# Hybrid encoder trunk: row norms tile by tile with the root on GpSimd, transposes by tile, table builds behind the first rows

## What is computed

```python
def _rmsnorm(x, g, eps=EPS):
    xf = x.astype(jnp.float32)
    y = xf * lax.rsqrt(jnp.mean(xf * xf, axis=-1, keepdims=True) + eps)
    return (y * g.astype(jnp.float32)).astype(x.dtype)

for l in range(DEPTH):
    h = _rmsnorm(x, norm_mix[l])
    x = x + (_even_mixer if l == 0 else _diff_attention)(h, ...)
    h = _rmsnorm(x, norm_ffn[l])
    x = x + _hier_moe(h, ...)     # 4 groups x 8 experts, top 2 of the best group
return _rmsnorm(x, norm_final)
```

## Time and profile before

| | us |
|---|---|
| median of 3 runs | 1727.0 (1726.47 to 1728.35) |
| the profiled execution's own time | 1730.77 |
| its span, first to last instruction | 1728.7 |
| PE busy | 1449.9 (84%) |
| DVE busy | 463.4 (27%) |
| ACT busy | 540.3 (31%) |
| POOL busy | 206.6 (12%) |
| DMA | 471.47 MB, mean 273 GB/s |
| chain that ended last, shares of the span | PE 48%, DMA 37%, DVE 7%, ACT 5% |

### The profile page before, as it was taken

One profiled execution on the slowest core, in us unless ns is written; L12 is line 12 of the kernel. 1 busy time (PEld: TensorE's weight loads), 2 busy tenths in 40 slices (PEclk: granted clock), 3 DMA queues, 4 the chain that ended last, 5 costly groups with the idle time before them and its releaser, 6 DMA issues.

```text
span 1728.7 us, 26191 instructions
## 1 busy us (share of the span) xinstructions
PE 1449.9 (84%) x9958; PEld 892.8 (52%) x9959; DVE 463.4 (27%) x983; ACT 540.3 (31%) x1013; POOL 206.6 (12%) x337
## 2 busy tenths in 40 slices
PE   4998994997887887884799898794997999879992
PEld 2875584553443443441688544482554555445551
DVE  4253734110110110112433587433110111101113
ACT  3334743221121121122422377632221222212222
POOL 3020000111111111110000000000211121111110
PEclk9999996998998998997899998996998999989996
DMA  3313036899999999995232100058999989999994
GB/s 142 105 68 123 2 122 246 333 405 404 413 410 407 412 407 406 413 404 197 71 97 97 60 33 22 25 215 307 403 417 406 395 340 422 423 413 401 396 383 165
DMA packets 67299, 471.47 MB, mean 273 GB/s; under 512 B 11368, under 2 KB 12392, under 8 KB 33456
## 3 DMA queue, kind: packets, MB, share of 16 engines
q1 hardware_dynamic: 52848, 438.73, 63.6%
q0 software_dynamic: 11520, 17.34, 3.0%
q10 hardware_dynamic: 2880, 14.68, 2.1%
HBM read 465.95 MB, written 25.20 MB: 284 GB/s over the span
## 4 chain that ended last, share of the span: by engine, by line
PE 48%; DMA 37%; DVE 7%; ACT 5%; issue 2%; SPq 0%; ACTq 0%; POOL 0%; DVEq 0%; POOLq 0%
DMA w<-in_w 30%; PE bank L374 17%; PE bank L748 15%; DMA xg<-hn_dram,icol 5%; PE bank L763 4%; PE bank L564 2%; PE bank L667 2%; DVE X L1381 1%; PE bank L647 1%; ACT HN L992 1%; PE bank L728 1%; DVE HN L1049 1%; PE bank L734 1%; DVE Pm L1235 1%; ACT Pm L944 1%
## 5 line engine op out<-in xcount | busy, mean ns | idle before, releaser
L748 PE MATMUL bank<-w,xT 128*64 128x256 f32 x4480 | 540.8, 403 | 104.7 <-DMA w<-in_w 103.0
L748 PEld LDWEIGHTS bank<-w,xT 128*64 128x64 f32 x4480 | 342.0, 146 | 326.5 <-issue 189.8
L1367 DVE TENSOR_TENSOR hh<-bank,sgate 64x256 f32<-64x256 f32 x140 | 59.6, 426 | 868.9 <-ACT sgate L1009 868.9
L763 PE MATMUL bank<-w,hT 128*64 128x512 f32 x1120 | 255.8, 598 | 0.0
L1009 ACT ACTIVATE sgate<-bank 64x256 f32<-64x256 f32 x140 | 52.7, 376 | 509.9 <-PE bank L748 509.9
L763 PEld LDWEIGHTS bank<-w,hT 128*64 128x64 f32 x1120 | 74.2, 136 | 124.7 <-issue 119.9
L333 ACT ACTIVATE whi<-raw 128x512 fp32r<-128x512 f32 (+1 forms) x112 | 67.4, 615 | 169.3 <-PE bank L374 168.8
L1016 ACT ACTIVATE ysb<-bank 128x512 f32<-128x512 f32 x70 | 41.8, 597 | 237.9 <-PE bank L763 237.9
L341 DVE TENSOR_TENSOR wlo<-raw,whi 128x512 fp32r<-128x512 f32 (+1 forms) x112 | 74.7, 679 | 149.2 <-ACT whi L333 149.2
L374 PE MATMUL bank<-whi,hi 128*128 128x512 f32 x224 | 90.8, 405 | 3.6 <-DVE wlo L341 3.6
L1009 ACT ACT_TABLE_LOAD x70 | 89.8, 1283 | 1.3
(11 more groups left out here) (225 smaller groups left out, 1485.0 us busy)
## 6 DMA issues: line engine op xcount, KB each, us to landing
w<-in_w SPq DMA_DIRECT2D x192, 2048.0 KB, 32.7
raw<-in_od_w_in SPq DMA_DIRECT2D x12, 1024.0 KB, 5.1
YG<-y_dram ACTq DMA_DIRECT2D x8, 1024.0 KB, 7.9
raw<-in_ev_w_in SPq DMA_DIRECT2D x6, 1024.0 KB, 5.1
raw<-in_ev_w_out SPq DMA_DIRECT2D x4, 1024.0 KB, 5.2
hn_dram<-HN ACTq DMA_DIRECT2D x8, 512.0 KB, 7.4
raw<-in_od_w_out SPq DMA_DIRECT2D x4, 1024.0 KB, 5.1
Wb<-line_dram SPq DMA_DIRECT2D x8, 448.0 KB, 3.6
```

The costliest lines, as they stand in the source:

```text
L748: last = pe.matmul(B[(1, 4)[c]][j * SLOT:j * SLOT + SLOT, 0:HH], xT[:, k, :], W13[s][:, j, k, c * HH:c * HH + HH], start=k == 0, stop=k == ...
L763: last = pe.matmul(B[3][j * SLOT:j * SLOT + SLOT, :], hT[:, k, :], W2[s][:, k, j * 512:j * 512 + 512], start=k == 0, stop=k == FK - 1)
L1367: dve.tensor_tensor(hh[:, c * HH:c * HH + HH].rearrange("q (a p) -> q a p", a=2), B[(1, 4)[c]][SLOT:P, 0:HH].rearrange("q (p a) -> q a p", ...
```

## The change

It touches the five row norms and the start. (1) `Square` gets a scale of D to the -1/2, so that its accumulator holds the mean square. The root is formed on POOL: add 1e-6, then the power -0.5 against a tile of constants, tile by tile at the first, third and fifth norm (`row_rstd`; s_sq, s_var2, s_row1) and for four columns at once in the routers. Ln and Exp and the dummy Ln go from ScalarE. (2) VectorE normalises each tile when its own factor is there; behind the expert stages these normalises (or final products) stand inside `combine`, one tile late. (3) Transposes run tile by tile; all eight chunks of the last tile signal. (4) The first dense group of each mixer waits for max(k + 1, 4) lo chunks; the bias-line products move behind chunk 5 of group 0. (5) CT gets its own semaphore, s_ct; PE's first wait is for it alone. (6) POOL's table builds wait for all eight lo chunks, and Wd is built in four parts; lambda products and cbf copies move behind groups 0 and 1 on VectorE.

```diff
-        def dense(pe, G, hi, lo, after=None, chunk=None):
+        def dense(pe, G, hi, lo, after=None, chunk=None, first=0, base=0):
...
                 if chunk:
-                    pe.wait_ge(chunk, k + 1)
+                    pe.wait_ge(chunk, base + max(k + 1, first))
...
-            sp.dma_start(CT[:, :], consts).then_inc(s_const, 16)
+            sp.dma_start(CT[:, :], consts).then_inc(s_ct, 16)
...
-                            sp.wait_ge(s_rstd, 3)
+                            sp.wait_ge(s_row1, TT + 1)
...
-            pe.wait_ge(s_const, 32)
+            pe.wait_ge(s_ct, 16)
...
-                for k in range(KD):
-                    for t in range(TT):
-                        if k == 0:
-                            pe.wait_ge(s_hn, TT * i + t + 1)
+                for t in range(TT):
+                    pe.wait_ge(s_hn, TT * i + t + 1)
+                    for k in range(KD):
                         last = pe.transpose(B[k][:, t * P:t * P + P], HN[:, t, k * P:k * P + P], ident)
-                    last.then_inc(s_htps, 1)
+                        if t == TT - 1:
+                            last.then_inc(s_htps, 1)
...
-                pe.wait_ge(s_lo, KD)
-                pe.wait_ge(s_bkt, 16)
-                for j in range(2):
-                    pe.matmul(B[6 + j][0:8, :], par("relb")[0:32, :], bkt[:, j * 512:j * 512 + 512], start=True, stop=True
-                              ).then_inc(s_line_mm, 1)
+                def bias_line():
+                    pe.wait_ge(s_lo, KD)
+                    pe.wait_ge(s_bkt, 16)
+                    pe.wait_ge(s_const, 16)
+                    for j in range(2):
+                        pe.matmul(B[6 + j][0:8, :], par("relb")[0:32, :], bkt[:, j * 512:j * 512 + 512], start=True, stop=True
+                                  ).then_inc(s_line_mm, 1)
...
-                for G in range(4):
+                dense(pe, 0, hi0, lo0, {5: bias_line}, s_lo, 4)
+                for G in range(1, 4):
                     dense(pe, G, hi0, lo0, {3: kv_transposes} if G == 2 else None)
-                pe.wait_ge(s_wd, 1)
+                pe.wait_ge(s_wd, 4)
...
-                pe.wait_ge(s_lo, 2 * KD)
-                for G in range(NB_L0, NB_L0 + 6):
+                dense(pe, NB_L0, hi1, lo1, None, s_lo, 4, KD)
+                for G in range(NB_L0 + 1, NB_L0 + 6):
...
-                if i:
-                    act.activation(tabw[:, 0:1], cst("eps6"), ACT.Ln)
                 for t in range(TT):
                     act.wait_ge(*ready(t))
-                    act.activation(HN[:, t, :], X[:, t, :], ACT.Square, accum_out=stats[:, t:t + 1]).then_inc(s_sq, 1)
+                    act.activation(HN[:, t, :], X[:, t, :], ACT.Square, scale=D ** -0.5, accum_out=stats[:, t:t + 1]).then_inc(s_sq, 1)
...
-                act.activation(stats[:, 4:8], stats[:, 0:4], ACT.Ln, scale=1.0 / D, bias=cst("eps6")).then_inc(s_sq, 1)
-                act.wait_ge(s_sq, (TT + 1) * (i // 2 + 1))
-                act.activation(stats[:, 8:12], stats[:, 4:8], ACT.Exp, scale=-0.5).then_inc(s_rstd, 1)
...
-                act.activation(tabw[:, 0:1], cst("eps6"), ACT.Ln)
                 for t in range(TT):
                     squares(l, 1, t)
-                act.wait_ge(s_rsum, l + 1)
-                act.activation(stats[:, 4:8], stats[:, 0:4], ACT.Ln, scale=1.0 / D, bias=cst("eps6")).then_inc(s_rln, 1)
-                act.wait_ge(s_rln, l + 1)
-                act.activation(stats[:, 8:12], stats[:, 4:8], ACT.Exp, scale=-0.5).then_inc(s_rstd, 1)
-                act.wait_ge(s_rstd, 2 * l + 2)
+                act.wait_ge(s_rstd, l + 1)
...
             def normalise(i):
-                dve.wait_ge(s_rstd, i + 1)
-                for t in range(TT):
+                for t in range(TT):
+                    dve.wait_ge(s_row1, TT * (i // 2) + t + 1)
                     dve.tensor_scalar(HN[:, t, :], X[:, t, :], stats[:, 8 + t:9 + t], None, ALU.mult).then_inc(s_hn, 1)
...
+            def normalise_tile(l, t):
+                dve.wait_ge(s_row1, TT * (l + 1) + t + 1)
+                if l == 0:
+                    dve.tensor_scalar(HN[:, t, :], X[:, t, :], stats[:, 8 + t:9 + t], None, ALU.mult).then_inc(s_hn, 1)
+                else:
+                    dve.wait_ge(s_gfin, 16)
+                    dve.scalar_tensor_tensor(out=HN[:, t, :], in0=X[:, t, :], scalar=stats[:, 8 + t:9 + t], in1=gfin[:, :],
+                                             op0=ALU.mult, op1=ALU.mult).then_inc(s_hn, 1)
...
                         dve.scalar_tensor_tensor(out=X[:, t, :], in0=YG[:, 2 * t + j, :], scalar=wgt[:, t, j:j + 1], in1=X[:, t, :],
                                                  op0=ALU.mult, op1=ALU.add).then_inc(s_mo[l], 1)
+                    if t:
+                        normalise_tile(l, t - 1)
+                normalise_tile(l, TT - 1)
...
+            pool.memset(neghalf[:, :], -0.5).then_inc(s_zero0, 1)
+            def row_rstd(i):
+                for t in range(TT):
+                    n = TT * (i // 2) + t + 1
+                    pool.wait_ge(s_sq, n)
+                    pool.tensor_scalar(stats[:, 4 + t:5 + t], stats[:, t:t + 1], 1e-6, None, ALU.add).then_inc(s_var2, 1)
+                    pool.wait_ge(s_var2, n)
+                    pool.tensor_tensor(stats[:, 8 + t:9 + t], stats[:, 4 + t:5 + t], neghalf[:, 0:1], ALU.pow).then_inc(s_row1, 1)
+            pool.wait_ge(s_zero0, 3)
+            row_rstd(0)
+            pool.wait_ge(s_lo, KD)
...
-            pool.tensor_tensor(Wd[:, :, :, :].rearrange("p j w c -> p (j w) c"), bcast(par("convw"), 32),
-                               cst("dia32").unsqueeze(1).broadcast_to([P, 4 * CONV_W, 32]), ALU.mult).then_inc(s_wd, 1)
+            for j in range(4):
+                pool.tensor_tensor(Wd[:, j, :, :], bcast(par("convw")[:, j * CONV_W:(j + 1) * CONV_W], 32),
+                                   cst("dia32").unsqueeze(1).broadcast_to([P, CONV_W, 32]), ALU.mult).then_inc(s_wd, 1)
...
-                pool.tensor_tensor(stats[:, 0:4], stats[:, 0:4], stats[:, 12:16], ALU.add).then_inc(s_rsum, 1)
+                pool.tensor_tensor(stats[:, 0:4], stats[:, 0:4], stats[:, 12:16], ALU.add).then_inc(s_rln, 1)
+                pool.wait_ge(s_rln, 2 * l + 1)
+                pool.tensor_scalar(stats[:, 4:8], stats[:, 0:4], 1e-6, None, ALU.add).then_inc(s_rln, 1)
+                pool.wait_ge(s_rln, 2 * l + 2)
+                pool.tensor_tensor(stats[:, 8:12], stats[:, 4:8], neghalf[:, :], ALU.pow).then_inc(s_rstd, 1)
...
             experts(0)
-            pool.wait_ge(s_rstd, 3)
+            row_rstd(2)
+            pool.wait_ge(s_row1, 2 * TT)
             pool.memset(kz1[:, :, :, :], 0.0).then_inc(s_kzz, 1)
```

More of the change, by code:

```diff
@@ L98, in build @@
         lamt = keep.take("lamt", [P, 8])
+        neghalf = keep.take("neghalf", [P, TT])
         tabw = keep.take("tabw", [P, 1])
@@ L527, in early_logits, with transposes @@
                 return hooks
-            def transposes(i, after=None):
-                for k in range(KD):
-                    for t in range(TT):
-                        if k == 0:
-                            pe.wait_ge(s_hn, TT * i + t + 1)
+            def transposes(i):
+                for t in range(TT):
+                    pe.wait_ge(s_hn, TT * i + t + 1)
+                    for k in range(KD):
                         last = pe.transpose(B[k][:, t * P:t * P + P], HN[:, t, k * P:k * P + P], ident)
-                    last.then_inc(s_htps, 1)
-                    if after and k in after:
-                        after[k]()
+                        if t == TT - 1:
+                            last.then_inc(s_htps, 1)
             def mixer0():
                 transposes(0)
-                pe.wait_ge(s_lo, KD)
-                pe.wait_ge(s_bkt, 16)
-                for j in range(2):
-                    pe.matmul(B[6 + j][0:8, :], par("relb")[0:32, :], bkt[:, j * 512:j * 512 + 512], start=True, stop=True
-                              ).then_inc(s_line_mm, 1)
+                def bias_line():
[5 more added lines that the diff above has]
+                                  ).then_inc(s_line_mm, 1)
                 def kv_transposes():
@@ L1034, in _ @@
         def _(dve):
-            dve.wait_ge(s_const, 32)
-            lp = par("lam").rearrange("p (j d) -> p j d", j=4)
-            for j in range(2):
-                dve.tensor_tensor_reduce(out=(ssum, rsum)[j][:, :], in0=lp[:, 2 * j, :], in1=lp[:, 2 * j + 1, :], scale=1.0, scalar=0.0,
-                                         op0=ALU.mult, op1=ALU.add, accum_out=lamt[:, j:j + 1]).then_inc(s_lam, 1)
-            for j, name in enumerate(("tri", "ones", "triexp")):
-                w = C_COLS[name][1]
-                dve.tensor_copy(cbf[:, j, 0:w], cst(name)).then_inc(s_cbf, 1)
             def normalise(i):
-                dve.wait_ge(s_rstd, i + 1)
                 for t in range(TT):
+                    dve.wait_ge(s_row1, TT * (i // 2) + t + 1)
```

(13 more changed lines are left out.)

19 lines of the change are left out of this document (9 added, 10 removed).

## The result

Five executions of the changed kernel gave a median of 1716.45 us (1715.62 to 1720.34), five of the kernel before 1727.26 us (1726.47 to 1728.35), on one chip and in turn. The ratio is 0.9943 [0.9929, 0.9957]: faster by 9.8 us, or by 10.8 us between the medians. The forecast was 1711 us. The sign was right and two thirds of the gain came; the median is 5.4 us above the forecast, at the upper edge of the range (1706 to 1716.5).

A forecast was written before the change was run, and what follows sets the result against it. PE's first projection matmul waited behind VectorE's normalise, held by POOL's Wd build; DMA was 97% busy in the expert stages. Start 11.4, routers -0.1 and 1.2, seam 1.6, end 1.8: 1727.0 - 15.9 = 1711 us, range 1706 to 1716.5.

The forecast's parts named there:

- The start: Kernel start to the convolution: first projection matmul at 22.5 instead of 35.65, bias products delay PE 1.7; gain 11.4 us.
- slow first stretch: Projection's first 3.6 us run at granted clock 0.50, expected the same in both kernels.
- pow at 0.3 us: POOL's root in all five norms: pow taken at 0.3 us, bounded by 0.20 and 1.01 us.
- POOL pow rows over 1 us: Sign that the forecast is wrong: pow instructions on POOL longer than 1 us in the trace.
- the end: Last combine and final products: root 3 at 1722.3, final 3 at 1723.5 instead of 1725.3; gain 1.8 us.
- The seam: First expert stage to second mixer: last normalise still collides with the kz MEMSET; gain 1.6 us, 3.2 without collision.
- no-collision rival: MEMSET loses to the normalise, adds not held: 1.6 us at the seam, 0.6 at the end, 1708.5 us; chance 0.10.
- The routers' table load: Exp load of 1.28 us ahead of the first router's softmax Exp: net -0.1 us; second router has none, +1.2.
- Slow pow: Rival at all five norms: gain gone from pow 2.7 us on; at 4 us the time is 1737; chance 0.03.
- late first pow: Rival at the start: first pow stalls by up to 7.31 us, transposes end 3.5 later, 1714.5 us; chance 0.07.
- Start lost: Rival: wlo late or attention paced elsewhere, so only routers, seam and end gain; 1722.5 us; chance 0.06.
- Four differences: Rival at the start: waiting for four differences, not eight, starts matmuls 2.7 us earlier, 1708 us; chance 0.02.

The follow-up runs named there:

- first profile: The changed kernel's first profiled execution, no further edit: 1718.53 us, span 1716.4 us.
- the second execution of before: The kernel before run and profiled once more, no edit: 1728.27 us.
- the two timings: The changed kernel timed twice, no edit between: medians 1716.45 us (ratio 0.9943) and 1719.39 us (ratio 0.9955).
- the combined kernel: Changed kernel with ScalarE forming the last norm's roots for tiles 2 and 3, kz memset behind mixer 1's transposes, Exp preloaded ahead of router squares: 1711.6 us, ratio 0.9914.

## Why the prediction was right in sign and short in size

*The start (11.4 forecast, 10.7 to 11.8 measured): right, step by step.* The root of the last tile was out at 11.24 (10.8), the fourth normalise ended at 12.0 (forecast 11.5), the first hi copy began at 15.55 (15.75), the differences ended at 21.7 (21.8), the first matmul came at 22.40 (22.5), the bias products took 1.81 us (1.7), and no wait followed in groups 0 to 3. The step took the slow first stretch to be the same in both kernels. It was not the same even between executions of one kernel: two differ by 1.1 us at the convolution, of the 1.5 us that the range allowed for the clock. The first profile's 11.8 us beat the forecast by 0.4 us, and 0.3 of them are luck: 3.0 us at 0.50 behind the first projection matmul, where the kernel before had 3.7. The 3.9 us of slack for the normalises swallowed pow's excess, as it was meant to.

*The failed step: pow at 0.3 us.* "I take 0.3 us, near the add, since form and size are the same and only arithmetic per element comes on top." The pow measured 0.57 us for 128x1 and 1.05 us for 128x4, where the same engine's add takes 0.22 and 0.23. The arithmetic, taken as a small extra, was most of the cost, and it grew with the columns, which the add's did not. The 1.05 us lie just above even the upper bound of 1.01, and "POOL pow rows over 1 us" was one of the prediction's signs of being wrong. It cost 0.75 us at each router: 1.2 became 0.39 in the second, and -0.1 became -0.9 in the first, whose table load (forecast at 1.28, measured 1.28) was otherwise right. Pow's excess is not all of it at the end: 0.3 us there, with 0.3 more because the add was held to 0.56 us beside the product of tile 2.

*The missing step: the end was priced to the last product only.* "3. ... root 3 at 1722.3, final 3 at 1723.5 instead of 1725.3. Gain 1.8 us" stops there. What lies between the last product and the span's end was taken over unchanged, with the engine that does the last work changed. The products gained 1.2 us and the tail lost 2.1. In all the end cost 0.9 us where 1.8 were to be won: the largest single miss, 2.7 of the 4.1 us. The trace of before held the row that would have shown it, GpSimd's drain of 7.76 us from 1698.82, in a record that none of the views lists. Its end, 6.54 us behind POOL's last instruction, and 0.2 us more to the span's end, set behind the forecast's own root 3 at 1722.3, give 1729.0 instead of 1723.5 + 3.4 = 1726.9: the 2.1 us that were measured. The question that was wanted is "which engine's last instruction do I move, and what does it still do afterwards".

*The seam (1.6 forecast, 1.44 measured; 1.05 against the second execution of before): right in its mechanism, near in its number partly by luck.* The port collision was there (2.38 us, had 2.375) and cost the 1.6 us that the no-collision rival gave to it. The last normalise ended only 0.4 us earlier against the first add (0.85 forecast), and what stands behind it gained 1.0 (0.8). The forecast reckoned with a held POOL add, but not with held pows: beside VectorE's two-input adds the pow took up to 1.65 us and the add up to 1.23, against 0.57 and 0.22 alone, and each pow that met such an add ended 0.4 us behind it (tile 1: 809.14 and 808.71). The Trainium skill (SBUF — State Buffer, Who interferes with whom) says that a VectorE instruction with two SBUF inputs contends with a GpSimd instruction that reads SBUF. This trace agrees.

*The routers' table load.* Taking the load off the first router's path brought 1.27 us, which is the load alone. The Trainium skill (ScalarE: Activation LUTs, What ACT_TABLE_LOAD costs) has 2.66 us for a switch; by that figure the kernel would have gained 1.4 us more there. The measurement decides.

*The rivals.* Slow pow as a loser needed 2.7 us and did not come; its milder form is what happened. A late first pow: the first took 0.57 us, at 6.11. The Trainium skill (GPSIMD Engine Reference, Instruction dispatch) has about 6 us on the first call of a freshly loaded kernel; no run here shows it for this instruction. Start lost: no. No collision: no, but one added wait makes it true. Four differences: shown idle.

*What stays open.* The sum over the measured stretches gives 11.8 us, the two timings 10.8 and 8.4 us between medians. The medians of the changed kernel differ by 3 us from one timing to the next (1716.45 and 1719.39), and the expert stages by 1 to 2 us between executions; no run here tells why.

## What to carry to other kernels

Find the collision before rearranging the work around it: one added wait on POOL had 8 of the start's 11 to 12 us. When the last instruction of an engine moves towards the end of a kernel, price what that engine still does after it, and let an engine that closes slowly finish early; the combined kernel got 2.6 us at the end from the same idea by giving only the first two tiles to POOL. A figure for an operation that the trace doesn't show should not be taken from another operation of the same shape: the pow took 2.6 times the add for one column and 4.6 times for four.

## What the runs showed of the hardware

- GpSimd's closing drain took 6.75 to 8.03 us in all 14 profiles. It began just ahead of POOL's last instruction and ended 6.54 to 6.56 us behind that instruction's end, whatever it was (a pow, a copy, a DMA issue); the span ended 0.2 us behind the later of GpSimd's and SP's drains. Behind the last product it cost 2.1 us, and 3.6 us with a copy still later.
- Pow on GpSimd: 0.57 us for 128x1 and 1.05 us for 128x4; an add 0.22 and 0.23. Beside VectorE instructions with two SBUF inputs up to 1.65 and 1.23 us; VectorE's adds kept their 1.28 us.
- After PE had idled ahead of the projection, the clock stayed at 0.50 until about 25.4 us in one execution and until about 28.2 in another of the same kernel, with the same work. Each microsecond more at 0.50 cost half a microsecond up to the convolution.
